# A two-layer transformer trunk on one core: the start-up loads of tokens and constants leave SyncE's DMA queue for ScalarE's

## The reference

```python
for l in range(DEPTH):
    mod_x = (jax.nn.silu(c) @ w_ada[l] + b_ada[l])[:, None, :]
    mod_c = (jax.nn.silu(c_ctx) @ w_ada[l] + b_ada[l])[None, None, :]
    ...
    x, ctx = hybrid_layer(x, ctx, mod_x, mod_c, p, lam_init, rope, need_ctx_out=(l < DEPTH - 1))
return rmsnorm(x, g_final)

def ffn_sublayer(s, m, i, g, wg, wu, wd):
    h = modulate(rmsnorm(s, g), m[3 * i], m[3 * i + 1])
    return s + 0.5 * m[3 * i + 2] * swiglu(h, wg, wu, wd)
```

## Time and profile before

| what | value |
|---|---|
| median of 3 runs | 2836.54 us (2836.24 to 2841.76) |
| the profiled execution's own time | 2838.13 us |
| its span, first to last instruction | 2836.2 us |
| TensorE busy | 96% of the span |
| VectorE, ScalarE, GpSimd busy | 59%, 27%, 7% |
| mean granted clock of TensorE | 0.983 |

### The profile page before, as it was taken

One profiled execution on the slowest core, in us unless ns is written; L12 is line 12 of the kernel. 1 busy time (PEld: TensorE's weight loads), 2 busy tenths in 40 slices (PEclk: granted clock), 3 DMA queues, 4 the chain that ended last, 5 costly groups with the idle time before them and its releaser, 6 DMA issues.

```text
span 2836.2 us, 38296 instructions
## 1 busy us (share of the span) xinstructions
PE 2715.3 (96%) x15352; PEld 2307.2 (81%) x15352; DVE 1687.2 (59%) x2403; ACT 763.9 (27%) x1131; POOL 197.8 (7%) x324
## 2 busy tenths in 40 slices
PE   6999999999987999999999999999999988899998
PEld 4888888888955878888888788888887956888887
DVE  5655655668837375656556756556348845544445
ACT  4211212133147232111121412111124155322222
POOL 2000000030003210000001200000002013100001
PEclk7999999999999999999999999999999999999999
DMA  7532333321111132333322233323122111132221
GB/s 269 177 121 89 104 104 92 97 79 60 45 47 43 45 104 90 116 106 98 109 89 89 81 98 104 104 93 128 45 70 65 60 60 39 54 116 89 89 89 45
DMA packets 180757, 255.35 MB, mean 90 GB/s; under 512 B 5311, under 2 KB 128813, under 8 KB 180653
## 3 DMA queue, kind: packets, MB, share of 16 engines
q1 hardware_dynamic: 180652, 253.90, 27.8%
HBM read 251.78 MB, written 2.10 MB: 90 GB/s over the span
## 4 chain that ended last, share of the span: by engine, by line
PE 89%; DVE 5%; ACT 2%; POOL 2%; SPq 1%; issue 1%; DMA 0%; DVEq 0%; POOLq 0%; ACTq 0%
PE ps L931 27%; PE ps L932 27%; PE ps L933 27%; PE ps L1322 1%; PE ps L1346 1%; PE ps L1267 1%; POOL sqsum L922 1%; DVE nb L2142 1%; DVE h_lo L1785 1%; PE ps L1334 1%; ACT e L1639 1%; PE ps L1072 1%; ACT w_hi L1419 1%; DVE rstd L1764 1%; POOL w_lo L834 0%
## 5 line engine op out<-in xcount | busy, mean ns | idle before, releaser
L931 PE MATMUL ps<-h_hi,w_hi 128*128 128x512 f32 (+1 forms) x3040 | 1048.9, 345 | 18.7 <-DVE h_lo L1785 17.5
L933 PE MATMUL ps<-h_hi,w_lo 128*128 128x512 f32 (+1 forms) x3040 | 1042.6, 343 | 0.0
L932 PE MATMUL ps<-h_lo,w_hi 128*128 128x512 f32 (+1 forms) x2928 | 1007.1, 344 | 0.0
L931 PEld LDWEIGHTS ps<-h_hi,w_hi 128*128 128x128 f32 x3040 | 582.2, 192 | 91.6 <-issue 19.4
L933 PEld LDWEIGHTS ps<-h_hi,w_lo 128*128 128x128 f32 x3040 | 581.6, 191 | 66.1
L932 PEld LDWEIGHTS ps<-h_lo,w_hi 128*128 128x128 f32 x2928 | 561.2, 192 | 64.7 <-issue 1.5
L1884 DVE TENSOR_TENSOR prod<-sil,ps 128x512 f32<-128x512 f32 (+1 forms) x156 | 87.9, 568 | 640.3 <-PE ps L933 633.3
L931 PE MATMUL ps<-hid_hi,w_hi 128*128 128x512 f32 (+1 forms) x1248 | 432.9, 347 | 0.0
L932 PE MATMUL ps<-hid_lo,w_hi 128*128 128x512 f32 (+1 forms) x1248 | 429.2, 344 | 0.0
L933 PE MATMUL ps<-hid_hi,w_lo 128*128 128x512 f32 (+1 forms) x1248 | 429.0, 344 | 0.0
L1419 ACT ACTIVATE w_hi<-raw 128x2048 fp32r<-128x2048 f32 x158 | 297.1, 1907 | 470.9 <-PE ps L933 470.9
(11 more groups left out here) (157 smaller groups left out, 1970.2 us busy)
## 6 DMA issues: line engine op xcount, KB each, us to landing
side_raw<-in_w_ada SPq DMA_DIRECT2D x120, 512.0 KB, 3.7
raw<-in_w_ffn_gate SPq DMA_DIRECT2D x44, 1024.0 KB, 5.3
raw<-in_w_ffn_up SPq DMA_DIRECT2D x44, 1024.0 KB, 5.3
raw<-in_w_ffn_down SPq DMA_DIRECT2D x44, 1024.0 KB, 4.9
raw<-in_w_in SPq DMA_DIRECT2D x14, 1024.0 KB, 5.3
ada_buf<-in_w_ada SPq DMA_DIRECT2D x9, 1024.0 KB, 10.5
raw<-in_w_out SPq DMA_DIRECT2D x8, 1024.0 KB, 5.1
raw<-in_w_in SPq DMA_DIRECT2D x8, 512.0 KB, 5.2
```

What stands on the lines that cost most here:

```text
L931: mm(out, wh, xh, start=start, stop=False)
L932: mm(out, wh, xl, start=False, stop=False)
L933: return mm(out, wl, xh, start=False, stop=stop)
```

## The change

The DMAs of the context and latent tokens, `vecc`, `sel`, `vec0`, `vec1`, `lams` and the taps are taken out of SyncE's list and put, in the same order, at the head of ScalarE's list. SyncE's list then begins with the identity and the six halves of blocks 0 to 2, with the first weight tile behind. Destinations and semaphores stay as they are. The DMA scratch is set to 1024 bytes.

```diff
@@ -689,17 +689,7 @@
         @block.sync
         def _(sp):
-            def load_tokens(t, landed):
-                src = a["x"][0, 128 * t:128 * t + 128, :] if t < 4 else a["ctx"][0, 128 * (t - 4):128 * (t - 4) + 128, :]
-                sp.dma_start(xnat[:, t, :], src).then_inc(landed, 16)
-
             sp.dma_start(ident[:], a["ident"]).then_inc(ident_landed, 16)
-            for t in (4, 5):
-                load_tokens(t, ctx_landed)
-            for src, dst in ((a["vecc"], vstage[0:3 * KD, 2, :]), (a["sel"], sel[:])):
-                sp.dma_start(dst, src).then_inc(cond_landed, 16)
-            for t in range(4):
-                load_tokens(t, x_landed)
...
             for b in BEFORE[:3]:
                 for half in range(2):
                     load_ada(b, half)
-                if b == 0:
-                    for src, dst in ((a["vec0"], vstage[0:NROW, 0, :]), (a["vec1"], vstage[0:NROW, 1, :]),
-                                     (a["lams"].broadcast_to((128, DEPTH * 4 * HD)), lamv[:].rearrange("p l i n -> p (l i n)"))):
-                        sp.dma_start(dst, src).then_inc(const_landed, 16)
-                    sp.dma_start(tapstage[:], a["vecw"]).then_inc(taps_landed, 16)
@@ -1696,6 +1681,16 @@
+            for t in (4, 5):
+                act.dma_start(xnat[:, t, :], a["ctx"][0, 128 * (t - 4):128 * (t - 4) + 128, :]).then_inc(ctx_landed, 16)
+            for src, dst in ((a["vecc"], vstage[0:3 * KD, 2, :]), (a["sel"], sel[:])):
+                act.dma_start(dst, src).then_inc(cond_landed, 16)
+            for t in range(4):
+                act.dma_start(xnat[:, t, :], a["x"][0, 128 * t:128 * t + 128, :]).then_inc(x_landed, 16)
+            for src, dst in ((a["vec0"], vstage[0:NROW, 0, :]), (a["vec1"], vstage[0:NROW, 1, :]),
+                             (a["lams"].broadcast_to((128, DEPTH * 4 * HD)), lamv[:].rearrange("p l i n -> p (l i n)"))):
+                act.dma_start(dst, src).then_inc(const_landed, 16)
+            act.dma_start(tapstage[:], a["vecw"]).then_inc(taps_landed, 16)
             take_vector(3, ccol[:].rearrange("p i k -> p (i k)"))
@@ -2314,7 +2309,7 @@
-    nc = bacc.Bacc("TRN2", target_bir_lowering=False, num_devices=1)
+    nc = bacc.Bacc("TRN2", target_bir_lowering=False, num_devices=1, dynamic_dma_scratch_size=1024)
```

## The result

The changed kernel takes 2852.48 us in the median of 5 runs against 2836.24 us: ratio 1.0054, 95% interval 1.0043 to 1.0065, slower. Repeated later beside other runs of the kernel before, it took 2851.26 against 2836.95 us, ratio 1.0052 (1.0038 to 1.0065). The forecast was 2848.7 us, 12.2 us later, in a range of 2835 to 2858; the medians of the first comparison lie 16.2 us apart, those of the repeat 14.3. The profiled execution took 2852.27 us, its span is 2850.5, 14.3 over the span before.

What follows compares the result with a forecast made beforehand. The start of TensorE's steady products was taken as the bound, with SyncE's queue standing behind one engine holding all vector rows. 2836.2 + 12.2 (26.6 - 14.4) = 2848.4 us span, 2848.7 against the runs' median; range 2835 to 2858.

Steps and rivals of the forecast that it cites:

- Step 1: SyncE loses the vector loads: fuller start gains 0.8 us, bounds 0 and 4.3 us.
- P: Start of TensorE's steady products, the matmul after the last wait for `h_lo`; 55.76 us in the kernel before.
- the rival with the hole as the bound: Fifteen engines starving at 16 to 22 us limit block 3; filling that gains 4.3 us: 2832.2, chance 8%.
- step 4: The sum: 26.6 - 14.4 = 12.2 us later, without the 0.8 us gain; block 3 waits for TensorE, other late landings covered.
- Step 2: ScalarE's work queues behind its 12 DMAs: P moves by F - 14.4 us, not at all when F is under 14.4.
- F: Time the taps are handed over on ScalarE's queue; TensorE's turn of block 0 can start at F + 18.1.
- The slack: Delay absorbed between TensorE's turn of block 0 and the steady products, at TensorE's and VectorE's waits; taken as 2.2 us.
- Step 3: F = 26.6 us, lower bound 13.8, with ScalarE's and SyncE's queues taking turns row by row on each DMA engine.
- The rule of about 110 rows of room: A load is accepted when the one before it fits with roughly 110 rows in the engine's queue; an estimate.
- The rival with equal bytes: The two queues share DMA engines equally by bytes: F = 23, 8.8 us later, 2845.3; chance 12%.
- that of whole loads: The two queues take turns by whole loads: F near 37, 22 us later, 2859; chance 8%.
- Step 5: Scratch of 1 KB moves all tiles down by 15 KB per partition: cost 0, within 1.7 us either way.

Runs made afterwards that it cites:

- Experiments 4: Changed kernel with vec0 and vec1 padded with zeros from 107 to 112 rows: 2833.90 against 2837.80 us for the kernel before, ratio 0.9984.
- experiment 5: Kernel before, all loads on SyncE, with vec0 and vec1 padded to 112 rows: 2834.02 against 2838.10 us, ratio 0.9988.
- its repeat: Kernel before with vectors of 112 rows, run once more with more rounds: 2832.74 against 2836.95 us, ratio 0.9985.
- Experiment 3: Changed kernel with vec0, vec1, lams and the taps back on SyncE behind block 0: 2836.27 against 2837.80 us for the kernel before, ratio 0.9995.
- experiments 6: Changed kernel, but SyncE waits for the latent tokens to land before issuing block 0: 2838.44 against 2838.10 us for the kernel before, ratio 1.0002.
- 2 (16.19: Changed kernel with only lams and the taps back on SyncE behind block 0: 2840.46 against 2837.80 us for the kernel before, ratio 1.0010.
- experiment 1: Kernel before with only the DMA scratch set to 1024 bytes: 2837.77 against 2837.80 us, ratio 1.0001.

## Why the prediction was right

**What bounds the kernel, and the one engine.** Right. Experiments 4 and 5 take the 107 rows off one engine; most of the standing goes (0.98 and 3.19 us at the vectors are left), and with it 4 us of the kernel before. The second price, that the same rows delay block 3, is shown by experiment 5 and its repeat, where its second half lands at 39.21 and 40.90 instead of 43.36.

**Step 1, the credit of 0.8 us** for two queues. Experiment 3 has this credit by itself: block 3 lands 1.0 us sooner and P is 0.9 us sooner, from one profile each; the medians alone don't tell it from no change. The fuller start is there as well (408 GB/s from 4 to 7 us, where the kernel before had 284). The Trainium skill, DMA: Bandwidth & Descriptors, section on issuing engines, says that several issuers save only the issue time. By experiment 3 the trace agrees: SyncE hands over block 0's first half at 1.60 there, before it was 5.81. The upper bound of 4.3 us, the rival with the hole as the bound, is not tested by experiment 3, where the hole remains. The changed kernel tests it: the hole is filled, the vectors are still on one engine, and block 3's second half lands at 40.48. That is 2.9 us sooner than before, so the 0.8 was too small for the landing (42.5 was forecast) and the 4.3 too large. The forecast does not hang on it, as step 4 said, because TensorE comes to block 3 only at 56.56.

**Step 2, P moves by F - 14.4.** With the measured F of 27.8 it gives 13.4; P moved by 14.4. The missing 1.0 is the clock. The turn of block 0 starts at 45.95, where F + 18.1 gives 45.9, so all of it lies behind. The slack was taken as 2.2 us, and two pieces ate part of it: the turn of block 1 took 1.87 us instead of 1.25, and the sums took 2.91 instead of 1.54, of which VectorE's reciprocals absorb 0.9, since the second no longer stands behind the first. In the repeat, with full clock there, P moved from 55.76 to 68.73, 13.0, where F = 27.87 gives 13.5. By experiments 6 (F = 13.83, P + 0.4) and 2 (16.19, P + 1.6, with the sums at full clock) the point from which it counts is right within a microsecond too. The place was named rightly: ScalarE's first copy near 28 (29.12), `part` near 44 (45.32), products near 68 (70.14), block 0's matmuls near 30 (31.28).

**Step 3, F = 26.6**, was the largest unknown, and turns row by row was the right one of three. The vector rows 0.10 us apart show it. It was put at 27.80 - 26.6 = 1.2 us too early. By turns the tokens were to be done at 14.7; their last row starts at 15.76, 1.1 us later. From 2 to 4 us the engines moved 275 GB/s at a busy share of 0.77, which the sum had left out and which makes about half a microsecond; the rest is not assigned. From there `lams` was to be accepted after 103 vector rows, 10.9 us; it was accepted at 27.30 after 114 of them, 11.5 us. The rule of about 110 rows of room holds: 100 vector rows and the 8 of `lams` were then left on the engine. The taps came 0.5 us behind `lams` instead of 1.0. The rival with equal bytes falls (the tokens and their partners got 65% and 38% of the engines' time, not half each). So does that of whole loads. The Trainium skill, DMA: Bandwidth & Descriptors, section on queues, rings and completion order, says that an engine drains a packet, typically 9 to 17 descriptors, before it switches. The trace does not agree: here the two queues went one row to one row.

**Step 4**, the covers, held: `lams` landed at 37.1 for VectorE and nobody else waited for it. One cover was named and not costed: TensorE stood 8.12 us before the last latent column, for the bank of ScalarE's first copy; the Silu behind it covers that.

**Step 5**, scratch: 0 by experiment 1.

In all, 12.2 us were forecast, and 14.3 (repeat) and 16.2 us (first comparison) measured; P moved by 14.4, of which 1.2 us are F and 1.0 the clock that the sum lacked. The direction and the mechanism hold. What would have improved the sum is the start-up rate, and a range of 1.4 us for where TensorE's clock comes back, which two executions of the same kernel leave open.

## What to carry to other kernels

A DMA instruction costs its issuer little (0.36 to 0.72 us each for the first eight here) only as long as there is room for it; behind a full engine it holds back everything in the issuer's list. Move loads to a compute engine's queue only after looking for loads whose rows all go to one engine (107 rows here), and give those a row count that spreads; that alone was worth 4 us here, more than any placement of the loads that was tried. And where two queues run at once, count rows, not bytes: small rows in one queue get the pace of large rows in the other.

## What the runs showed that I had not expected

SyncE's queue of blocks could start 10.6 us later at almost no cost (experiment 6, P + 0.4 us against the kernel before). That holds for a ScalarE that starts at 15.15; whether the blocks have as much room behind one that starts at 10.9, as with 112 rows, no run shows. And with identical loads, TensorE's clock in the stretch of the sums came back in one execution and not in the other (1.54 and 2.91 us), worth 1.4 us at the products.
